# Two low-rank products of a recurrent block put side by side on the array, with half of a projection between them

## The chip, the cores and the metric

The kernel runs on one NeuronCore of a Trainium2 chip. The metric is the time of one execution on the device in microseconds (us). A profile is one execution in which every instruction's start and length were recorded. PE is TensorE (PEld its weight loads), DVE is VectorE, ACT is ScalarE, POOL is GpSimd, SP is SyncE, whose queue starts nearly all transfers.

## What is computed

A model of two blocks in a row, float32 throughout, 256 tokens of width 1024. The second block has a layer of attention, a mixture of 32 experts, a recurrent layer (RWKV-7 time mixing) and a second mixture of experts. The change lies in the first part of the recurrent layer. Cut to what matters:

```python
def rwkv7_time_mix(x, mu, w_rkv, w_o, w0, w1, w2, a0, a1, a2, g1, g2, k_k, k_a, r_k, ...):
    xx = jnp.pad(x, ((0, 0), (1, 0), (0, 0)))[:, :-1] - x
    xm = x[None] + xx[None] * mu[:, None, None, :]            # six mixed inputs
    r, k, v = jnp.einsum('nbsd,nde->nbse', xm[:3], w_rkv)     # 1024 -> 1024 each
    xv, xw, xa, xg = xm[2], xm[3], xm[4], xm[5]
    w = -jax.nn.softplus(-(w0 + jnp.tanh(xw @ w1) @ w2)) - 0.5   # decay: 1024 -> 64 -> 1024
    a = jax.nn.sigmoid(a0 + (xa @ a1) @ a2)                      # learning rate: 1024 -> 64 -> 1024
    g = jax.nn.sigmoid(xg @ g1) @ g2                             # gate: 1024 -> 160 -> 1024
    kk = (k * k_k).reshape(B, S, H, N)
    kk = kk / jnp.maximum(jnp.sqrt(jnp.sum(kk * kk, -1, keepdims=True)), 1e-12)
    k = k * (1.0 + (a - 1.0) * k_a)
    ...                                                       # then the recurrence over time
```

## The kernel before

One instruction stream for each engine is written out by hand, in the order in which it runs. `tensor_program`, `vector_program`, `scalar_program`, `gpsimd_program` and `sync_program` each have a function `rwkv` or a part for this layer. Engines wait for each other by counting semaphores: an instruction that ends something others need gets a name ("rw lw1"), and `wait_ge(*act("rw lw1"))` waits until ACT has come to that name. Nothing is reordered: an engine that waits holds up all that stands behind in its stream.

**PSUM.** TensorE's results go to four tiles of 128 x 1024 (ps0 to ps3), which are handed out in turn by `tile(name, ...)`. The tile handed out is waited for until the engine that reads its former content has done so. Each "half" of a product (512 of the 1024 outputs, as four blocks of 128 outputs by 256 tokens) fills one such tile.

**The stretch in question on TensorE (before).** k0, k1 (the k projection, two halves of 32 matmuls 128x128 by 128x256) come first. Then "rw w" is 8 matmuls of 128 inputs by 64 outputs on the array's columns 0 to 63. "rw a" is 8 alike on columns 64 to 127. Then come the second factors, "rw lw0", "rw lw1" (decay, 64 inputs on the array's rows 0 to 63) and "rw aT0", "rw aT1" (learning rate, rows 64 to 127), with four matmuls each. Then r0 and r1 (the r projection), the sums of squares "rw norm", the gate's first factor "rw g", the product "rw kk0/kk2" which spreads the norms, the gate's second factor "rw gt0/gt1", "rw bon", and half of the v projection, "rw v0". One fp32 matmul makes two MATMUL records in the trace.

**ACT.** It copies k0, k1; takes tanh of w and copies a into `r.loT`; scales k into `r.kk` by 8 instructions; then 16 sigmoids (lw0, lw1, aT0, aT1, four each); copies r0 and r1; takes the square root of the norms ("rw ln"); the gate's sigmoids; three exponentials; and further copies.

**DVE.** It makes the mixed inputs (`mix(i, dst)`: 8 instructions each). mix 0 (for r) overwrites the buffer `r.xa` from which k is computed, so it waits for "rw k1". mix 5 and mix 2 overwrite the inputs of w and a. Then, in its stream in this order:

```python
        v.wait_ge(*act("rw aT1"))
        for k in range(KT):
            ts(ka3[:, k, :], aT[:, k, :], vcol("ka", k), r.om[:, k:k + 1], MUL, ADD)
        tt(flat(kT), v_, flat(kT), MUL)
        for k in range(KT):
            after_own()
            v.tensor_tensor_scan(Lc[:, k, :], tab["rst"], lw[:, k, :], 0.0, MUL, ADD).then_inc(*dve.one())
        tt(flat(lw), flat(Lc), flat(lw), SUB, "rw decay")
        ln = xx[:, 0:2, :]
        v.wait_ge(*pe("rw norm"))
        ts(ln, two(ps("rw norm"), 256), 1e-24, None, MAX, None, "rw norm")
        v.wait_ge(*act("rw ln"))
        rec(ln, ln, "rw ln")
```

TensorE's "rw kk0" waits for this last "rw ln" of DVE.

Of the kernel before, what the change touches and what calls it, by code (L numbers as in the profile page):

```python
# [13 lines left out]
P = 128  # L14
# [3 lines left out]
KT = 8  # L18
# [379 lines left out]
def tensor_program(t, m):  # L398
# [3 lines left out]
    ps = m.ps  # L402
    ps.restart()

    def mm(lst, name=None):
        for n, (o, l, r, first, last) in enumerate(lst):
            i = t.matmul(o, l, r, start=first, stop=last, skip_group_check=True)  # L407
            if n == len(lst) - 1:
                i.then_inc(*pe.one(name))
# [14 lines left out]
    def tile(name, *free):  # L424

        p, old = ps.take(name, *free)
        for engine, done in old:
            t.wait_ge(*engine(done))
        return p
# [642 lines left out]
    def rwkv():  # L1072
# [4 lines left out]
            tr([(p[:, (k % 4) * 256 + i * P:(k % 4) * 256 + i * P + P], x[:, i, k * P:(k + 1) * P], idn)  # L1077
                for k in range(4 * half, 4 * half + 4) for i in range(NT)], n)

        def proj(name, ready, src):  # L1080
            for half in range(2):
                n = f"rw {name}{half}"
                p = tile(n, (act, n))
                t.wait_ge(*m.w.landed(n))
                t.wait_ge(*dve(ready))
                mm(proj_T(wcols(m.w(n), KT, 512), src, KT, [(p[:, c * 256:(c + 1) * 256], slice(c * P, (c + 1) * P)) for c in range(4)]), n)
# [5 lines left out]
        p = tile("rw wa", (act, "rw wa out"))  # L1092
        t.wait_ge(*m.w.landed("rw lora1"))
        t.wait_ge(*dve("rw mix3"))
        mm([(p[0:64, 0:256], lv[:, k, 0:64], r.xb[:, k, :], k == 0, k == 7) for k in range(KT)], "rw w")
        t.wait_ge(*dve("rw mix4"))
        mm([(p[64:128, 512:768], lv[:, k, 64:128], r.xc[:, k, :], k == 0, k == 7) for k in range(KT)], "rw a")
        for base, n_ in ((0, "lw"), (64, "aT")):
            for half in range(2):
                n = f"rw {n_}{half}"  # L1100
                p = tile(n, (act, n))
                t.wait_ge(*act("rw wa out"))
                t.wait_ge(*m.w.landed("rw lora2"))
                mm([(p[:, c * 256:(c + 1) * 256], lora2[base:base + 64, (4 * half + c) * P:(4 * half + c + 1) * P],
                     r.loT[base:base + 64, :], True, True) for c in range(4)], n)
        proj("r", "rw mix0", r.xa)
        sq3 = flat(r.gt).rearrange("p (k s) -> p k s", k=KT)
        p = tile("rw norm", (dve, "rw norm"))
        t.wait_ge(*dve("rw kk2"))
# [217 lines left out]
def vector_program(v, m):  # L1327
# [591 lines left out]
    def rwkv():  # L1919
# [19 lines left out]
        ka3 = v_.rearrange("p (k s) -> p k s", k=KT)  # L1939
        v.wait_ge(*act("rw kk"))  # L1940
        tt(g_, flat(kk), flat(kk), MUL, "rw kk2")
        v.wait_ge(*pe("rw w"))
        mix(5, r.xb)
        v.wait_ge(*pe("rw a"))
        mix(2, r.xc)
        ts(r.om, m.vec[:, m.VO["ka"]:m.VO["ka"] + 8], -1.0, 1.0, MUL, ADD)
        v.wait_ge(*act("rw aT1"))
# [152 lines left out]
def scalar_program(s, m):  # L2100
# [351 lines left out]
    def rwkv():  # L2452
        r = m.rw
        B = blocks(m)
        s.wait_ge(*pe("rw in0"))
        cp(m.hT[:, 0:4, :], ps("rw in0").rearrange("p (k s) -> p k s", k=4), "rw in0 out")

        def proj_out(name, dst):
            for half in range(2):
                n = f"rw {name}{half}"  # L2460
                s.wait_ge(*pe(n))
                cp(dst[:, 4 * half:4 * half + 4, :], ps(n).rearrange("p (k s) -> p k s", k=4), n)

        proj_out("k", r.kT)
        p = ps("rw wa")
        s.wait_ge(*pe("rw w"))
        fn(r.loT[0:64], p[0:64, 0:256], ACT.Tanh)
        s.wait_ge(*pe("rw a"))
        cp(r.loT[64:128], p[64:128, 512:768], "rw wa out")
        for k in range(KT):  # L2470
            fn(r.kk[:, k, :], r.kT[:, k, :], ACT.Copy, "rw kk" if k == KT - 1 else None, scale=vcol("kk", k))
        for n_, dst, bias in (("lw", r.lw, "w0"), ("aT", r.aT, "a0")):
            for half in range(2):
                n = f"rw {n_}{half}"
                s.wait_ge(*pe(n))
                for c in range(4):
                    fn(dst[:, 4 * half + c, :], ps(n)[:, c * 256:(c + 1) * 256], ACT.Sigmoid, n if c == 3 else None,
                       bias=vcol(bias, 4 * half + c))
        proj_out("r", r.rT)
        ln, sg = r.xx[:, 0:2, :], r.xx[:, 2:4, :]  # L2480
        s.wait_ge(*dve("rw norm"))
        fn(ln, ln, ACT.Sqrt, "rw ln")
        p = ps("rw g")
        s.wait_ge(*pe("rw g"))
        s.wait_ge(*dve("rw mix2"))
        fn(sg[:, 0, :], p[:, 0:256], ACT.Sigmoid)
        fn(sg[0:32, 1, :], p[0:32, 256:512], ACT.Sigmoid, "rw g out")
        dec = -math.exp(-0.5)
        s.wait_ge(*dve("rw decay"))
        fn(flat(r.vt), flat(r.Lc), ACT.Exp, "rw e1", scale=dec)  # L2490
        fn(flat(r.xb), flat(r.Lc), ACT.Exp, "rw e3", scale=-dec)
        fn(flat(r.lw), flat(r.lw), ACT.Exp, "rw e2", scale=dec)
        for i in range(NT):
            s.wait_ge(*pe(f"rw gt{i}"))
            cp(r.gt[:, i, :], ps(f"rw gt{i}"), f"rw gt{i}")
        s.wait_ge(*dve("rw pc"))
        for half in range(2):
            n = f"rw v{half}"
            s.wait_ge(*pe(n))
            cp(r.vt[:, :, 512 * half:512 * half + 512], ps(n).rearrange("p (t n) -> p t n", t=NT), n)  # L2500

        def out(i, n, dst, mark=" out"):
            s.wait_ge(*pe(f"rw{i} {n}"))
            cp(dst, ps(f"rw{i} {n}"), f"rw{i} {n}{mark}")

        def powers(i, step):

            s.wait_ge(*pe(f"rw{i} pw{step} d"))
            out(i, f"pw{step} n", B[i]["n"])
            out(i, f"pw{step} d", B[i]["d"])  # L2510

        for i in range(NT):
            s.wait_ge(*pe(f"rw{i} sq d"))
            s.wait_ge(*m.pool(f"rw{i} X"))
            out(i, "sq n", B[i]["n"])
            out(i, "sq d", B[i]["d"])
        for i in range(NT):
            powers(i, 1)
        for i in range(NT):
            out(i, "mv", B[i]["mv"])  # L2520
        for i in range(NT):
            powers(i, 2)
        for i in range(NT):
            out(i, "T0 n", B[i]["n"])
            out(i, "T0 d", B[i]["d"])
        for i in range(NT):
            out(i, "ktok", B[i]["ktok"], "")
        for i in range(NT):
            out(i, "T1", B[i]["n"])
        for i in range(NT):  # L2530
            out(i, "atok", B[i]["atok"], "")
            out(i, "btok", B[i]["btok"], "")
        for i in range(NT):
            out(i, "U", B[i]["U"])
        for i in range(NT):
            s.wait_ge(*pe(f"rw{i} G"))
            w = 1024 >> i
            cp(B[i]["G"][:, 0:w], ps(f"rw{i} G")[:, 0:w], f"rw{i} G")
        for i in range(NT):
            out(i, "y0", m.hb[:, i, :], "")  # L2540

        def rms(i):
            s.wait_ge(*dve(f"rw o{i} ms"))
            fn(r.va[i], r.va[i], ACT.Sqrt, f"rw o{i} rms")

        for i in range(NT):
            rms(i)
            tile_out(f"rw oT{i}", r.kT, i)
        join("rw", range(NT))
# [325 lines left out]
```

## Time and profile before

| | |
|---|---|
| median of 3 runs | 2208.9 us (2207.1 to 2209.21) |
| the profiled execution: its own time | 2207.6 us |
| its span, first to last instruction | 2205.7 us |
| PE busy | 1796.1 us, 81% of the span |
| DVE busy | 603.0 us, 27% |
| ACT busy | 392.2 us, 18% |
| mean granted TensorE clock | 0.917 of full |

Busy time is the time in which an engine has an instruction in work. The span leaves out some 2 us of launch and end, which the own time has. The stretch in question begins 1399 us after the span's start.

### The profile page before, as it was taken

What the parts mean: (1) busy time and instruction counts of PE and PEld (TensorE: products, weight loads), DVE (VectorE), ACT (ScalarE), POOL (GpSimd) and SP (SyncE); (2) the same over time, 40 slices, a digit from 0 to 9 for tenths busy, and PEclk for the clock granted to TensorE, in tenths of its full rate; (3) what the DMA queues carried; (4) which work ended last, traced back from release to release, by engine and by line L of the source; (5) the groups of instructions that cost most, each with busy time, mean ns of one, the idle gap of its engine ahead of it and who ended that gap; (6) DMA issues with size and microseconds to landing.
All of it is one profiled execution on the core that took longest, in us unless ns stands there. A gap on an engine that the chain in (4) does not pass through costs nothing.

```text
span 2205.7 us, 30929 instructions
## 1 busy us (share of the span) xinstructions
PE 1796.1 (81%) x13574; PEld 1129.6 (51%) x13574; DVE 603.0 (27%) x1013; ACT 392.2 (18%) x755; POOL 16.9 (1%) x18
## 2 busy tenths in 40 slices
PE   6999999999999987675766887699986677966663
PEld 4788884878886754222222332575983322322220
DVE  1133312123422145211111212464345321121102
ACT  2233211323301142100000001141221100100001
POOL 0000000000000000000000000001000000000000
PEclk9999999999999998988798998799997788989877
DMA  9322333333234434899999996213013899999995
GB/s 337 104 81 96 134 145 151 123 82 129 96 134 172 171 115 196 367 425 425 425 425 425 425 373 244 77 57 116 4 50 128 367 424 425 413 424 425 424 426 223
DMA packets 51162, 539.55 MB, mean 245 GB/s; under 512 B 7392, under 2 KB 16224, under 8 KB 17664
## 3 DMA queue, kind: packets, MB, share of 16 engines
q1 hardware_dynamic: 49248, 527.06, 58.7%
q0 software_dynamic: 864, 6.29, 0.8%
q8 instruction: 173, 2.83, 0.5%
q10 hardware_dynamic: 832, 3.00, 0.4%
q14 instruction: 45, 0.37, 0.0%
HBM read 535.28 MB, written 1.05 MB: 243 GB/s over the span
## 4 chain that ended last, share of the span: by engine, by line
PE 69%; DMA 18%; DVE 5%; issue 5%; ACT 3%; DVEq 0%; ACTq 0%
PE ps L407 53%; PE ps L414 13%; DMA arena<-in_moe_w_gu 10%; DMA arena<-in_moe_w_down 3%; DMA ring<-in_moe_w_down 3%; PE ps L420 3%; DMA ring<-in_moe_w_gu 1%; DVE x L1350 1%; ACT arena L2121 1%; DVE arena L1339 1%; ACT hb L2117 1%; DVE mT L1339 1%; ACT arena L2392 0%; ACT arena L2117 0%; DVE mT L1912 0%
## 5 line engine op out<-in xcount | busy, mean ns | idle before, releaser
L407 PE MATMUL ps<-hT,ring 128*128 128x256 f32 (+2 forms) x1888 | 392.5, 372 | 0.0
L407 PEld LDWEIGHTS ps<-hT,ring 128*128 128x128 f32 (+2 forms) x1888 | 330.8, 185 | 54.0 <-issue 3.4
L414 PE MATMUL ps<-arena 128*32 128x512 f32 (+1 forms) x1572 | 242.7, 703 | 107.5 <-issue 68.8
L414 PE MATMUL ps<-ring,arena 128*32 128x512 f32 x1472 | 210.6, 708 | 99.9 <-issue 72.9
L2121 ACT ACTIVATE arena<-ps 128x512 f32<-128x512 f32 (+4 forms) x143 | 93.4, 653 | 894.7 <-PE ps L414 518.5
L407 PE MATMUL ps<-arena 64*64 64x64 f32 (+10 forms) x1944 | 184.2, 320 | 57.0 <-ACT arena L2392 22.3
L1339 DVE TENSOR_TENSOR arena<-arena,ps 128x256 f32<-128x256 f32 (+2 forms) x82 | 46.0, 561 | 558.7 <-ACT arena L2117 466.6
L414 PEld LDWEIGHTS ps<-arena 128*32 128x32 f32 (+1 forms) x1572 | 64.0, 130 | 261.6 <-issue 204.2
L407 PEld LDWEIGHTS ps<-arena 64*64 64x64 f32 (+4 forms) x1944 | 113.5, 159 | 130.5 <-ACT arena L2392 52.8
L414 PEld LDWEIGHTS ps<-ring,arena 128*32 128x32 f32 x1472 | 54.8, 126 | 237.4 <-issue 194.2
L407 PE MATMUL ps<-ring,hT 128*128 128x256 f32 (+4 forms) x576 | 148.6, 416 | 8.7 <-ACT hT L2117 7.0
L407 PE MATMUL ps<-arena,ring 64*64 64x64 f32 (+2 forms) x1120 | 140.3, 299 | 10.8 <-DVE arena L1350 8.3
L407 PE MATMUL ps<-ring,arena 64*64 64x64 f32 (+3 forms) x1328 | 128.3, 310 | 13.7 <-issue 8.9
L407 PEld LDWEIGHTS ps<-arena,ring 64*64 64x64 f32 (+2 forms) x1120 | 122.5, 163 | 26.7 <-DVE arena L1350 8.7
L407 PEld LDWEIGHTS ps<-ring,hT 128*128 128x128 f32 x576 | 98.9, 192 | 50.8 <-issue 27.7
L1339 DVE TENSOR_TENSOR mT<-mT,ps 128x1024 f32<-128x1024 f32 x40 | 48.8, 1221 | 209.3 <-PE ps L407 209.2
L407 PEld LDWEIGHTS ps<-ring,arena 64*64 64x64 f32 (+3 forms) x1328 | 72.7, 137 | 62.6 <-issue 57.2
L407 PE MATMUL ps<-ring,mT 64*64 64x64 f32 (+1 forms) x704 | 73.5, 286 | 0.6 <-issue 0.6
L420 PE MATMUL ps<-tcom,arena 128*128 128x128 f32 (+1 forms) x370 | 53.8, 281 | 24.5 <-ACT arena L2121 24.5
L420 PEld LDWEIGHTS ps<-tcom,arena 128*128 128x128 f32 (+1 forms) x370 | 42.2, 143 | 61.5 <-issue 57.2
L2117 ACT ACT_TABLE_LOAD x50 | 64.2, 1283 | 44.7 <-DVE small L1344 18.8
L407 PE MATMUL ps<-arena,x 128*128 128x128 f32 x512 | 70.7, 298 | 1.5 <-DVE arena L1339 1.5
(162 smaller groups left out, 1231.2 us busy)
## 6 DMA issues: line engine op xcount, KB each, us to landing
ring<-in_moe_w_gu SPq DMA_DIRECT2D x64, 2048.0 KB, 28.6
arena<-in_moe_w_gu SPq DMA_DIRECT2D x64, 2048.0 KB, 30.9
arena<-in_moe_w_down SPq DMA_DIRECT2D x32, 2048.0 KB, 32.9
ring<-in_moe_w_down SPq DMA_DIRECT2D x32, 2048.0 KB, 31.5
ring<-in_w_merge SPq DMA_DIRECT2D x16, 2048.0 KB, 7.7
ring<-in_w_in SPq DMA_DIRECT2D x10, 2048.0 KB, 7.3
ring<-in_attn_w_qkv SPq DMA_DIRECT2D x6, 2048.0 KB, 7.5
ring<-in_rw_w_rkv SPq DMA_DIRECT2D x6, 2048.0 KB, 7.5
```

The source lines that it names most:

```text
L407: i = t.matmul(o, l, r, start=first, stop=last, skip_group_check=True)
L414: i = t.matmul(o, l, r, start=first, stop=last, skip_group_check=True)
L420: i = t.transpose(o, a, e)
L1339: v.tensor_tensor(o, a, b, op).then_inc(*dve.one(name))
L1350: v.scalar_tensor_tensor(out=o, in0=a, scalar=s, in1=b, op0=op0, op1=op1).then_inc(*dve.one(name))
L2117: s.activation(o, a, f, **k).then_inc(*act.one(name))
L2121: s.activation(o, a, ACT.Copy).then_inc(*act.one(name))
```

## The change

On TensorE: the 16 matmuls of w and a alternate between the two halves of the array's columns, under one name "rw wa". r0 comes right behind them. Then lw0 and aT0 are handed two tiles at once, and their matmuls alternate between the two halves of the rows; then lw1 and aT1 the same way; then r1. DVE and ACT wait for "rw wa" where they waited for "rw w" and "rw a". ACT takes its work in a new order: copy r0, sigmoids lw0 and aT0, copy r1, sigmoids lw1 and aT1.

```diff
-        def proj(name, ready, src):
-            for half in range(2):
+        def proj(name, ready, src, halves=range(2)):
+            for half in halves:
...
         p = tile("rw wa", (act, "rw wa out"))
         t.wait_ge(*m.w.landed("rw lora1"))
         t.wait_ge(*dve("rw mix3"))
-        mm([(p[0:64, 0:256], lv[:, k, 0:64], r.xb[:, k, :], k == 0, k == 7) for k in range(KT)], "rw w")
         t.wait_ge(*dve("rw mix4"))
-        mm([(p[64:128, 512:768], lv[:, k, 64:128], r.xc[:, k, :], k == 0, k == 7) for k in range(KT)], "rw a")
-        for base, n_ in ((0, "lw"), (64, "aT")):
-            for half in range(2):
-                n = f"rw {n_}{half}"
-                p = tile(n, (act, n))
-                t.wait_ge(*act("rw wa out"))
-                t.wait_ge(*m.w.landed("rw lora2"))
-                mm([(p[:, c * 256:(c + 1) * 256], lora2[base:base + 64, (4 * half + c) * P:(4 * half + c + 1) * P],
-                     r.loT[base:base + 64, :], True, True) for c in range(4)], n)
-        proj("r", "rw mix0", r.xa)
+
+        mm([o for k in range(KT) for o in ((p[0:64, 0:256], lv[:, k, 0:64], r.xb[:, k, :], k == 0, k == 7),
+                                           (p[64:128, 512:768], lv[:, k, 64:128], r.xc[:, k, :], k == 0, k == 7))], "rw wa")
+        proj("r", "rw mix0", r.xa, (0,))
+        for half in range(2):
+
+            ns = [f"rw {n_}{half}" for n_ in ("lw", "aT")]
+            ps_ = [tile(n, (act, n)) for n in ns]
+            t.wait_ge(*act("rw wa out"))
+            t.wait_ge(*m.w.landed("rw lora2"))
+            mm([(o[:, c * 256:(c + 1) * 256], lora2[base:base + 64, (4 * half + c) * P:(4 * half + c + 1) * P],
+                 r.loT[base:base + 64, :], True, True) for c in range(4) for base, o in zip((0, 64), ps_)], ns[0])
+            pe.name(ns[1])
+        proj("r", "rw mix0", r.xa, (1,))
...
         tt(g_, flat(kk), flat(kk), MUL, "rw kk2")
-        v.wait_ge(*pe("rw w"))
+        v.wait_ge(*pe("rw wa"))
         mix(5, r.xb)
-        v.wait_ge(*pe("rw a"))
         mix(2, r.xc)
...
         p = ps("rw wa")
-        s.wait_ge(*pe("rw w"))
+        s.wait_ge(*pe("rw wa"))
         fn(r.loT[0:64], p[0:64, 0:256], ACT.Tanh)
-        s.wait_ge(*pe("rw a"))
         cp(r.loT[64:128], p[64:128, 512:768], "rw wa out")
         for k in range(KT):
             fn(r.kk[:, k, :], r.kT[:, k, :], ACT.Copy, "rw kk" if k == KT - 1 else None, scale=vcol("kk", k))
-        for n_, dst, bias in (("lw", r.lw, "w0"), ("aT", r.aT, "a0")):
-            for half in range(2):
+        def r_out(half):
+            n = f"rw r{half}"
+            s.wait_ge(*pe(n))
+            cp(r.rT[:, 4 * half:4 * half + 4, :], ps(n).rearrange("p (k s) -> p k s", k=4), n)
+
+        for half in range(2):
+            r_out(half)
+            for n_, dst, bias in (("lw", r.lw, "w0"), ("aT", r.aT, "a0")):
                 n = f"rw {n_}{half}"
                 s.wait_ge(*pe(n))
                 for c in range(4):
                     fn(dst[:, 4 * half + c, :], ps(n)[:, c * 256:(c + 1) * 256], ACT.Sigmoid, n if c == 3 else None,
                        bias=vcol(bias, 4 * half + c))
-        proj_out("r", r.rT)
         ln, sg = r.xx[:, 0:2, :], r.xx[:, 2:4, :]
```

The order on ACT before, from the 8 scalings of k to the square root ("rw ln", 128x512). The rows of 128x256 from ps are the sigmoids of lw0, lw1, aT0 and aT1, four each; the two of 128x1024 are the copies of r0 and r1.

```order
L2117 ACTIVATE arena<-arena,vec 128x256 [waits act_done] x8
L2117 ACT_TABLE_LOAD [waits act_done]
L2117 ACTIVATE arena<-ps,vec 128x256 [waits pe_done]
L2117 ACTIVATE arena<-ps,vec 128x256 [waits act_done] x3
L2117 ACTIVATE arena<-ps,vec 128x256 [waits act_done,pe_done]
...
L2121 ACTIVATE arena<-ps 128x1024 [waits act_done,pe_done] x2
L2117 ACT_TABLE_LOAD [waits act_done]
L2117 ACTIVATE arena<-arena 128x512 [waits dve_done]
```

The same place on ACT after the change: the copy of r0, the table load, the sigmoids of lw0 and aT0, the copy of r1, and those of lw1 and aT1.

```order
L2119 ACTIVATE arena<-arena,vec 128x256 [waits act_done] x8
L2123 ACTIVATE arena<-ps 128x1024 [waits act_done,pe_done]
L2119 ACT_TABLE_LOAD [waits act_done]
L2119 ACTIVATE arena<-ps,vec 128x256 [waits pe_done]
...
L2119 ACTIVATE arena<-ps,vec 128x256 [waits act_done] x3
L2123 ACTIVATE arena<-ps 128x1024 [waits act_done,pe_done]
L2119 ACTIVATE arena<-ps,vec 128x256 [waits act_done,pe_done]
...
L2119 ACTIVATE arena<-ps,vec 128x256 [waits act_done] x3
L2119 ACT_TABLE_LOAD [waits act_done]
L2119 ACTIVATE arena<-arena 128x512 [waits dve_done]
```

One copy (r1) now stands ahead of eight of the sixteen sigmoids, and one (r0) ahead of them all; the number of table loads is as before.

On TensorE before, from the a product to r0, with the numbers of tiles (ps0 to ps3) and of weight buffers:

```order
L407 MATMUL ps0<-hb,ring0 64x256 x7
L407 MATMUL ps1<-arena,ring1 128x256 [waits ring_landed1,act_done,dve_done]
L407 MATMUL ps1<-arena,ring1 128x256 x3
L407 MATMUL ps2<-arena,ring1 128x256 [waits ring_landed1,act_done]
L407 MATMUL ps2<-arena,ring1 128x256 x3
L407 MATMUL ps3<-arena,ring1 128x256 [waits ring_landed1,act_done]
L407 MATMUL ps3<-arena,ring1 128x256 x3
L407 MATMUL ps0<-arena,ring1 128x256 [waits ring_landed1,act_done]
L407 MATMUL ps0<-arena,ring1 128x256 x3
L407 MATMUL ps1<-arena,ring2 128x256 [waits dve_done,ring_landed2,act_done]
L407 MATMUL ps1<-arena,ring2 128x256 x31
```

On TensorE after, from the last of the alternating w and a matmuls to r1; r0 is the one from ring2, r1 the one from ring3:

```order
L407 MATMUL ps0<-mT,ring0 64x256
L407 MATMUL ps0<-hb,ring0 64x256
L407 MATMUL ps1<-arena,ring2 128x256 [waits dve_done,ring_landed2]
L407 MATMUL ps1<-arena,ring2 128x256 x31
L407 MATMUL ps2<-arena,ring1 128x256 [waits act_done,ring_landed1]
L407 MATMUL ps3<-arena,ring1 128x256
...
L407 MATMUL ps0<-arena,ring1 128x256 [waits act_done,ring_landed1]
L407 MATMUL ps1<-arena,ring1 128x256
...
L407 MATMUL ps2<-arena,ring3 128x256 [waits dve_done,ring_landed3,act_done]
L407 MATMUL ps2<-arena,ring3 128x256 x31
```

r0 now takes ps1 and stands ahead of the second factors. lw0 and aT0 take ps2 and ps3, lw1 and aT1 ps0 and ps1, and r1 takes ps2, which it shares in turn with lw0. DVE's order is unchanged. The rows behind r1 (norm on ps3, g on ps0, kk0 on ps1, kk2 on ps2) are as before.

## Rows read from the trace of the kernel before

**Rows 1.** Chain that ended last, in the window 1380 to 1550 us: start, us, what.

```profile
1399.04 0.14 issue
1399.18 36.69 PE ps L407 x160
...
1444.01 67.20 PE ps L407 x424
```

**Rows 2.** Timeline of PE: start, us, engine, line, operation, records, [idle before, releaser].

```profile
1399.18 30.43 PE L407 MATMUL ps<-arena,ring 128*128 128x256 f32 x128 [8.34 <-DVE arena L1350]
...
1436.37 6.39 PE L407 MATMUL ps<-arena,ring 64*128 64x256 f32 x32 [0.52 <-issue]
1444.01 27.89 PE L407 MATMUL ps<-arena,ring 128*128 128x256 f32 x128 [1.25 <-ACT arena L2117]
1471.83 1.07 PE L407 MATMUL ps<-arena,tcom 128*32 128x256 f32 x16
1472.83 7.29 PE L407 MATMUL ps<-mT,ring 128*128 128x256 f32 x32
1480.06 1.16 PE L407 MATMUL ps<-arena,tcom 32*128 32x256 f32 x16
...
1493.21 15.62 PE L407 MATMUL ps<-ring,hb 128*128 128x512 f32 x32
```

**Rows 3.** Timeline of PE where w ends and a begins.

```profile
1429.54 3.02 PE L407 MATMUL ps<-mT,ring 128*64 128x256 f32 x13
...
1432.39 0.38 PE L407 MATMUL ps<-mT,ring 128*64 128x256 f32 x1
1432.45 0.38 PE L407 MATMUL ps<-hb,ring 128*64 128x256 f32 x1
1432.61 0.38 PE L407 MATMUL ps<-mT,ring 128*64 128x256 f32 x1
```

**Rows 4.** Timeline of ACT from the scalings of k to the square root.

```profile
1436.30 4.29 ACT L2117 ACTIVATE arena<-arena,vec 128x256 f32<-128x256 f32 x8
1440.67 1.28 ACT L2117 ACT_TABLE_LOAD   x1
1441.96 8.26 ACT L2117 ACTIVATE arena<-ps,vec 128x256 f32<-128x256 f32 x16
...
1471.94 1.02 ACT L2121 ACTIVATE arena<-ps 128x1024 f32<-128x1024 f32 x1 [12.79 <-PE ps L407]
...
1474.33 0.63 ACT L2117 ACTIVATE arena<-arena 128x512 f32<-128x512 f32 x1
```

**Rows 5.** Timeline of DVE from mix 0 to the end of its preparations.

```profile
1429.65 4.13 DVE L1350 SCALAR_TENSOR_TENSOR arena<-arena,vec,hT 128x256 f32<-128x256 f32 x8 [22.28 <-PE ps L407]
...
1451.69 3.56 DVE L1346 TENSOR_SCALAR arena<-arena,vec 128x256 f32<-128x256 f32 x8
...
1463.41 2.29 DVE L1339 TENSOR_TENSOR arena<-arena 128x2048 f32<-128x2048 f32 x1
1472.97 0.69 DVE L1344 TENSOR_SCALAR arena<-ps 128x512 f32<-128x512 f32 x1 [7.27 <-PE ps L407]
1474.99 3.35 DVE L1358 RECIPROCAL arena<-arena 128x512 f32<-128x512 f32 x1 [1.33 <-ACT arena L2117]
...
1497.83 2.29 DVE L1350 SCALAR_TENSOR_TENSOR arena<-arena 128x2048 f32<-128x2048 f32 x1
```

**Rows 6.** Windows: stretch, its length, busy by engine, PE clock, DMA share, GB/s.

```profile
1399.20:1404.40 5.20, 5.20 (x12) 4.16 (x13) 4.84 (x11) 0.00 (x0) 0.00 (x0) 0.50 0.01 3
1404.40:1429.50 25.10, 25.10 (x117) 21.85 (x115) 2.79 (x6) 1.02 (x1) 0.00 (x0) 1.00 0.22 84
1493.10:1496.50 3.40, 3.40 (x6) 1.61 (x7) 3.37 (x2) 0.00 (x0) 0.00 (x0) 0.50 0.88 376
```

**Rows 7.** The second mixture of experts: its window, in the same columns.

```profile
1700.00:2180.00 480.00, 333.93 (x2298) 131.68 (x2301) 93.29 (x187) 39.65 (x73) 0.00 (x0) 0.85 0.98 412
```

**Rows 8.** Timeline of SP's queue where those experts' transfers start.

```profile
1698.84 0.92 SPq L2634 DMA_DIRECT2D arena<-in_moe_w_down  x2
```

## Prediction

> **What bounds the kernel now.** I read first the chain of work that ended last, in the window of the recurrent layer. It is nearly all TensorE: 36.69 us from 1399.18, and 67.20 us without a break from 1444.01 [rows 1]. Between the two it goes over ACT: the copy of a, the scalings of k, the table load and the four sigmoids of lw0, for whose tile r0 waits [rows 4], while TensorE works through its 6.39 us of second factors [rows 2]. So a microsecond less or more of TensorE here moves all that follows. Behind the layer, the second mixture of experts runs with the transfers at 0.98 of their capacity [rows 7], and its stream starts at 1698.84 [rows 8], when the recurrent layer is over and its memory is lent. Nothing upstream of that waits for transfers, so a shift of the layer's end shifts the stream and the end of the kernel by the same amount. I then read the timelines of PE, ACT and DVE, since the change moves only instructions. On PE the reader is to see the stages in a row with gaps of 0.52 and 1.25 us [rows 2]. On ACT the 16 sigmoids run in one piece long before the r copies [rows 4]. On DVE a block of work that needs these sigmoids, the factor of k and the decay's running sums, runs from 1451.69 to 1465.70, followed by 7.27 us of waiting for the norms [rows 5]. That wait is the cushion between the sigmoids and TensorE's product kk0, which began at 1480.06 [rows 2].
>
> **The change on TensorE, up to r1.** Where w ends and a begins, the two happen to run together: w's records start at 1432.39 and 1432.61, a's at 1432.45 between them [rows 3]. That is a pair every 0.22 us, where r takes 27.89 us for 128 records, 0.218 each [rows 2]. So 16 records of w and 16 of a in pairs take 16 x 0.218 = 3.5 us, from 1429.54 to about 1433.1, where they ended at 1399.18 + 36.69 = 1435.87 before [rows 1]. r0 is next. It needs mix 0, which DVE ends at 1429.65 + 4.13 = 1433.78 [rows 5]; with 0.14 us between the end of a mix and a matmul, as ahead of k0 [rows 1], r0 starts at 1433.9. This is a new wait of 0.8 us, but the old one of 0.52 us for ACT's copy goes. Its 64 records end at 1433.9 + 13.95 = 1447.9. The 32 records of the second factors took 6.39 us [rows 2]; on two halves of the rows I take 16 pairs at 0.218, 3.5 us, until 1451.4. `r.loT` is long done by then, since ACT needs only a tanh and a copy for it behind 1433.1. The nearest row for different rows at once is kk0/kk2, 16 records on four row groups in 1.16 us [rows 2], which are 0.07 us each, so the pairing is not in doubt.
>
> r1 takes ps2, so it waits for ACT's sigmoids of lw0. ACT first copies r0 (1448.0 to 1449.1), then loads its table for 1.28 us (before, the load ran at 1440.67 right behind the scalings; now the copy stands ahead of it), then does four sigmoids of 0.516 us, 8.26/16 [rows 4]: done at 1452.5. So r1 starts at 1452.6, after 1.2 us of waiting, as much as the 1.25 us there was. It ends at 1452.6 + 13.95 = 1466.5, against 1471.9 before. **So far TensorE has won 5.4 us.**
>
> **What the new order on ACT does.** The copy of r1 now stands ahead of the sigmoids of lw1 and aT1. These two are ready in PSUM at 1451.4, but ACT waits for r1 until 1466.6, copies for 1.02 us, and does eight sigmoids of 0.516 us: lw1 is done at 1469.8, aT1 at 1471.8. Before, all 16 were done at 1441.96 + 8.26 = 1450.22 [rows 4]. The last one is 21.6 us later. Two things queue behind it.
>
> First, DVE. Its stream waits for aT1 before the block that took 14.0 us (1451.69 to 1463.41 + 2.29 [rows 5]). It now runs from 1471.9 to 1485.9. Only behind it stand the norms, although TensorE has them at 1467.6: 0.69 us for the maximum, ACT's root of 0.63 us [rows 4], and the reciprocal of 3.35 us [rows 5]. With some 0.04 us at each handover, that is 1486.6, 1487.3 and 1490.7. TensorE's kk0 starts at 1490.8 instead of 1480.06: **10.7 us later**.
>
> Second, TensorE itself. norm needs 1.07 us until 1467.6. g takes ps0, which lw1 had, and waits for ACT until 1469.8, 2.2 us, then runs 7.29 us until 1477.1 [rows 2]. Then TensorE is idle for 13.7 us, until 1490.8. The 2.2 us cost nothing since they lie inside that wait.
>
> Nothing behind kk is late in its turn. DVE needs 1500.12 - 1480.06 = 20.1 us from kk0's start to the end of its preparations (1497.83 + 2.29 [rows 5]), while TensorE goes through gt, bon and v0 for 28.8 us, until 1493.21 + 15.62 = 1508.83 [rows 2]. Both move by the same amount, so 8.7 us of cover remain. ACT's exponentials need DVE's decay, which at 1485.9 is ready 4.9 us before kk0 starts, and they stand behind the gate's sigmoids as before. v0's weights are asked for when g is done, at 1477, and are used at 1504. The root's table load stands behind the sigmoids and ends at 1473.2, before the norms come.
>
> **The clock.** A long idle time costs again behind it. After 8.34 us of idle with little before, k0 began at a granted clock of 0.50 (1.2 GHz) until 1404.40, then 1.00 (2.4 GHz) [rows 6]. The same 128 records took 30.43 us there and 27.89 in r [rows 2]: 2.5 us. An idle time of 13.7 us is nearer to that than to the 1.25 us ahead of r, which cost nothing, so I take 2.5 us for kk and gt. The bounds: nothing from below, and from above 2.5 plus another such stretch of 3.4 us at half clock, as at 1493.1 behind bon [rows 6], worth 1.7 us. That one is there already; it might also be missed, -1.7.
>
> **Sum.** 10.7 + 2.5 = 13.2 us later. Against the profiled execution's own 2207.6 us that is 2220.8; the median of the runs, 2208.9, lies 1.3 us above that execution, so 2222. The bounds are 10.7 - 1.7 = 9.0 (2218) and 10.7 + 2.5 + 1.7 = 14.9 (2224), and some 1.5 to 3 us for how the second experts' 480 us fall on the clock.
>
> **A rule that speaks against the pairs.** The row shows w's and a's matmuls, both on all 128 rows and on different columns, started 0.06 us apart [rows 3]. The Trainium skill, "TensorE: Matmul & The Clock Gate", Part 3, says that a weight load overlaps a running matmul only when the row groups differ. By that rule w and a would not run together, while the second factors would. By rows, w and a one after the other take 32 x 0.218 = 7.0 us and end at 1436.5, 2.7 us later than 1433.8, where r0 could start; all behind moves along, 15.9 us in all, 2225. The rule is contradicted by the trace of this case, so I give this 3 in 100.
>
> **Rivals.**
> The forecast, a stall of TensorE before kk because aT1's sigmoids stand behind r1: 2222, 0.84. Its own range is 2217 to 2226.
> (A) The gain arrives: kk0 starts right behind g. Then norm, g end at 1466.5 + 1.07 + 7.29 = 1474.8, 5.3 us earlier than 1480.1, 2204. For it speaks only that TensorE is the chain and wins 5.4 us. From aT1's end to kk0 DVE and ACT need 1490.8 - 1471.8 = 19.0 us, so aT1 would have to be done by 1455.8 for the whole gain, and 1461.1 is the point from which the time is not longer than before. ACT reaches aT1 at 1471.8 because the r1 copy is ahead of it. 0.03.
> (B) The stall is there but absorbed behind, by a wait that is there anyway: 2209, no change. Against it: the chain in the layer is unbroken TensorE [rows 1], and transfers of the experts start only when the layer ends [rows 8]. 0.04.
> (C) The pairs don't form, by the rule above: 2225, 0.03.
> (D) The stall takes more with it, a second slow-clock stretch in gt and v0, or later wait of DVE's: from 17 us, 2227 and more, 0.06.
>
> **How the numbers follow.** A run of this kernel differs from another by some 2 us, so within 0.2% (4.4 us) counts as no change. Faster has only (A), 0.03. The same has (B), 0.04. Slower has the rest, 0.93. The range 2217 to 2227 holds the forecast and (C); left out are A, B, most of D and the forecast's edge, together under 2 in 10.
>
> **What the changed profile would show.** w's and a's records alternate in pairs 0.22 us apart and r0 starts near 1433.9; the second factors take 3.5 us. r1 begins near 1452.6 with a wait of about 1.2 us for ACT. On ACT there is an idle time of some 12 us ahead of the second 128x1024 copy, with eight sigmoids behind it. DVE idles some 20 us until 1471.9, ahead of its 128x256 TENSOR_SCALARs. PE idles some 13.7 us before the 32-row matmuls at 1490.8, and the granted clock there is 0.5 for a few microseconds. The experts' transfers start near 1712. It would be wrong if ACT came to aT1 before r1, if DVE's norms did not stand behind the decay block, or if later waits shrank by as much as this one costs.

## Result, and the profile after

| | median | lowest to highest | runs |
|---|---|---|---|
| before | 2208.94 us | 2207.1 to 2209.21 | 4 |
| changed | 2230.58 us | 2227.95 to 2236.78 | 4 |

The ratio is 1.0104, with an interval of 1.008 to 1.0128: 21.6 us slower. On another chip, beside the experiments, it was 2227.05 us against 2206.82, ratio 1.0086 (1.0064 to 1.0108). The forecast was slower by 13, to 2222, and its range ended at 2227. The profiled execution took 2236.78 us, the longest of the four, with a span of 2234.8.

PE's timeline of the changed kernel, in the columns of [rows 2] (w's and a's last two records stand here for their 32):

```profile
1401.32 30.42 PE L407 MATMUL ps<-arena,ring 128*128 128x256 f32 x128 [8.34 <-DVE arena L1353]
...
1434.96 0.38 PE L407 MATMUL ps<-mT,ring 128*64 128x256 f32 x1
1434.97 0.38 PE L407 MATMUL ps<-hb,ring 128*64 128x256 f32 x1
1436.06 17.71 PE L407 MATMUL ps<-arena,ring 128*128 128x256 f32 x96 [0.71 <-DVE arena L1353]
1454.59 14.08 PE L407 MATMUL ps<-arena,ring 128*128 128x256 f32 x64 [0.82 <-ACT arena L2119]
1468.60 1.07 PE L407 MATMUL ps<-arena,tcom 128*32 128x256 f32 x16
1471.87 7.29 PE L407 MATMUL ps<-mT,ring 128*128 128x256 f32 x32 [2.20 <-ACT arena L2119]
1492.93 2.22 PE L407 MATMUL ps<-arena,tcom 32*128 32x256 f32 x16 [13.77 <-DVE arena L1361]
1495.08 16.10 PE L407 MATMUL ps<-ring,arena 128*128 128x512 f32 x16
1511.10 6.99 PE L407 MATMUL ps<-tcom,arena 128*128 128x2 f32 x32
```

The whole layer started 2.14 us later in this execution (k0 at 1401.32, before at 1399.18 [rows 2]), so places are compared from k0's start on. The reader is to see the three waits, 0.71 for mix 0, 0.82 for lw0's sigmoids and 2.20 for lw1's, and then 13.77 us of idle time ahead of kk0. Behind it everything takes nearly twice its time: kk 2.22 us for 1.16, gt 16.10 for 8.50, bon 6.99 for 3.78.

ACT's timeline there, where the copy of r1 stands between the two groups of eight sigmoids:

```profile
1450.15 1.02 ACT L2123 ACTIVATE arena<-ps 128x1024 f32<-128x1024 f32 x1 [9.65 <-PE ps L407]
1451.25 1.28 ACT L2119 ACT_TABLE_LOAD   x1
1452.54 4.08 ACT L2119 ACTIVATE arena<-ps,vec 128x256 f32<-128x256 f32 x8
1468.70 1.02 ACT L2123 ACTIVATE arena<-ps 128x1024 f32<-128x1024 f32 x1 [12.08 <-PE ps L407]
1469.82 4.08 ACT L2119 ACTIVATE arena<-ps,vec 128x256 f32<-128x256 f32 x8
```

And DVE's, from the block that waits for them to the reciprocal, against [rows 5]:

```profile
1473.93 3.56 DVE L1349 TENSOR_SCALAR arena<-arena,vec 128x256 f32<-128x256 f32 x8 [22.50 <-ACT arena L2119]
...
1485.65 2.29 DVE L1342 TENSOR_TENSOR arena<-arena 128x2048 f32<-128x2048 f32 x1
1488.05 0.69 DVE L1347 TENSOR_SCALAR arena<-ps 128x512 f32<-128x512 f32 x1
1489.43 3.35 DVE L1361 RECIPROCAL arena<-arena 128x512 f32<-128x512 f32 x1 [0.69 <-ACT arena L2119]
```

DVE waits 22.50 us for the sigmoids and no longer at all for the norms; the 7.27 us of cushion are gone. Windows of the changed kernel, in the columns of [rows 6]: g, the idle time, kk, gt, bon, and v0 up to and from the return of the clock.

```profile
1471.90:1479.10 7.20, 7.20 (x32) 4.60 (x32) 4.88 (x9) 3.18 (x5) 0.00 (x0) 1.00 0.01 2
1479.10:1492.90 13.80, 0.06 (x1) 0.00 (x0) 12.58 (x12) 3.91 (x5) 0.00 (x0) 0.59 0.40 152
1492.90:1495.00 2.10, 2.07 (x16) 1.52 (x16) 0.00 (x0) 2.06 (x3) 0.00 (x0) 0.50 0.00 0
1495.00:1511.10 16.10, 16.10 (x19) 4.00 (x16) 15.26 (x15) 4.74 (x3) 0.00 (x0) 0.50 0.00 0
1511.10:1517.90 6.80, 6.80 (x33) 6.80 (x33) 2.72 (x2) 1.02 (x1) 0.00 (x0) 0.50 0.80 308
1517.90:1522.60 4.70, 4.70 (x7) 2.12 (x8) 0.19 (x1) 0.00 (x0) 0.00 (x0) 0.50 0.00 0
1522.60:1534.20 11.60, 11.60 (x31) 4.88 (x31) 0.00 (x0) 0.00 (x0) 0.00 (x0) 1.00 0.00 0
```

The clock column stays at 0.50 through kk, gt, bon and the start of v0, 29.7 us from kk0's start, although TensorE is busy all that time. The forecast had some 5 us of it.

### The profile page after: what moved, and what is told of

Read it like the earlier page. It is cut to its first block, busy times and chain, and to the rows that moved or that the text cites. A ratio compares the mean times of both kernels' runs of the same rounds, so it can differ in the third digit from the quotient of the medians.

```text
span 2234.8 us, 30928 instructions
## 1 busy us (share of the span) xinstructions
PE 1815.6 (81%) x13574; PEld 1134.4 (51%) x13574; DVE 602.9 (27%) x1013; ACT 392.0 (18%) x755; POOL 16.9 (1%) x18
## 3 DMA queue, kind: packets, MB, share of 16 engines
HBM read 535.28 MB, written 1.05 MB: 240 GB/s over the span
## 4 chain that ended last, share of the span: by engine, by line
PE 67%; DMA 19%; DVE 6%; issue 5%; ACT 3%; DVEq 0%; ACTq 0%
PE ps L407 52%; PE ps L414 12%; DMA arena<-in_moe_w_gu 8%; DMA arena<-in_moe_w_down 6%; DMA ring<-in_moe_w_down 3%; PE ps L420 2%; DMA ring<-in_moe_w_gu 1%; DVE x L1353 1%; DVE arena L1342 1%; ACT arena L2123 1%; ACT hb L2119 1%; DVE mT L1342 1%; DVE arena L1353 1%; ACT arena L2394 0%; ACT arena L2119 0%
## 5 line engine op out<-in xcount | busy, mean ns | idle before, releaser
L407 PE MATMUL ps<-ring,arena 64*64 64x64 f32 (+3 forms) x1328 | 138.0, 325 | 12.6 <-issue 8.0
L407 PEld LDWEIGHTS ps<-ring,hT 128*128 128x128 f32 x576 | 100.7, 195 | 53.4 <-issue 30.5
L1365 DVE COPY arena<-ps 128x512 f32<-128x512 f32 (+7 forms) x60 | 36.3, 605 | 126.5 <-PE ps L407 116.3
```

The costliest lines, as they stand in the source:

```text
L1365: v.tensor_copy(o, a).then_inc(*dve.one(name))
```

## The experiments

Two theories stood at the outset. The first: aT1's sigmoids behind r1 make kk0 10.7 us late, and the slow clock which the idle time leaves makes up the rest. The rival: something else of the change costs, the pairs or a shift in the second experts. All profiles are put side by side here; the places count from k0's start (before: 1399.18). Medians are against the runs of before on the same chip: 2206.75 for e1 to e4, 2206.82 for e5 to e9, 2205.7 for e10 to e12, and 2208.94 for the first row of the changed kernel.

| kernel | idle ahead of kk0 | kk0 starts | from kk0 to v0 | oT0 starts | median, change to before |
|---|---|---|---|---|---|
| before | 0 | 80.9 | 13.2 | 263.7 | |
| changed (first profile) | 13.8 | 91.6 | 25.0 | 290.6 | +21.6 |
| e9 changed again | 13.8 | 91.6 | 25.0 | 289.8 | +20.2 |
| e1 sigmoids first | 2.95 | 78.5 | 23.6 | 273.6 | +2.6 |
| e2 pairs only | 0 | 80.4 | 15.7 | 266.4 | +3.1 |
| e3 filler | 0 | 90.4 | 14.8 | 278.9 | +19.9 |
| e10 filler, wide | 0 | 93.6 | 14.8 | 283.6 | +15.8 |
| e4 v0 ahead of gt | 13.8 | 90.5 | | 279.2 | +17.3 |
| e8 idle time alone | 3.41 | 84.7 | 25.0 | 280.3 | +15.4 |
| e7 pairs undone | 2.65 | 80.4 | 15.8 | 266.4 | +1.0 |
| e5 norms early | 0 | 75.5 | 14.5 | 259.6 | -5.5 |
| e12 the same, no pairs | 0 | 77.7 | 13.4 | 262.6 | -3.6 |

(e4 has v0 elsewhere. oT0 are the transposes that end the recurrence. The rows behind this table are PE's timelines of each kernel. In e3 and e4 the 128 records of k0 and k1 took 29.3 us instead of 30.4, so their places are some 1.1 us early in this count.)

The last column does not follow from the one ahead of it alone. From oT0 to the end of the span these profiles took 539.7 to 543.1 us, e3 546.5, in no order that follows the edits, and k0 itself started between 1396.0 and 1401.3. So a microsecond in the layer is read from the places, and a median is asked only for more than that.

**e1, the sigmoids ahead of r1's copy.**

```diff
-        for half in range(2):
-            r_out(half)
+        r_out(0)
+        for half in range(2):
             for n_, dst, bias in (("lw", r.lw, "w0"), ("aT", r.aT, "a0")):
...
+        r_out(1)
```

> The change with one thing undone: ACT does all 16 sigmoids ahead of the copy of r1 (the copy of r0 stays first). Theory (the loss comes from aT1's sigmoids standing behind r1 on ACT, and from the slow clock that the stall leaves): aT1 is done near 1456.7 us on the time axis of before, DVE's decay block ends at 1470.7, the norms and the reciprocal follow, kk0 starts at 1475.6 right behind g, without a long idle time and at full clock. 1475.6 against 1480.06: 4.5 us faster than before, about 2204.5. Rival (the pairs on the array or r0's new place cost something by themselves): slower than before by several us even so.

Measured: 2209.31 us (2200.91 to 2225.09, 12 runs), ratio 1.0014 (0.9993 to 1.0035): the large loss is gone with this one edit, but no gain was seen. Part of the number was my own slip: 16 sigmoids, not 8, stand between the table load and DVE, so aT1 is done at 1458.7, not 1456.7, and kk0 started at 78.5, which is 1477.7 on the axis of before and still 2.4 us early. But it started behind 2.95 us of idle time, and what follows is the surprise. PE's timeline and the windows of e1:

```profile
1478.73 1.27 PE L407 MATMUL ps<-arena,tcom 32*128 32x256 f32 x16 [2.95 <-DVE arena L1361]
1479.93 15.59 PE L407 MATMUL ps<-ring,arena 128*128 128x512 f32 x16
```

```profile
1478.70:1480.50 1.80, 1.77 (x18) 1.20 (x18) 0.60 (x1) 1.79 (x2) 0.00 (x0) 0.99 0.94 400
1480.50:1507.80 27.30, 27.30 (x55) 12.74 (x54) 17.57 (x17) 6.03 (x5) 0.00 (x0) 0.50 0.27 104
```

The clock fell 0.6 us into gt and stayed at half for 27.3 us of uninterrupted matmuls. From kk0 to v0 that is 23.6 us for 13.2, so this execution should end 10.4 - 2.4 = 8.0 us later than before, and its own time, 2215.32 us, is 8.6 above the median of before. The 24 us of spread over 12 runs would fit some runs with this and some without, but only the profiled one can be seen.

**e2, the pairs alone.** Before, with the two alternating lists, r0 and r1 behind them and ACT in its old order.

```diff
+        mm([o for k in range(KT) for o in ((p[0:64, 0:256], lv[:, k, 0:64], r.xb[:, k, :], k == 0, k == 7),
+                                           (p[64:128, 512:768], lv[:, k, 64:128], r.xc[:, k, :], k == 0, k == 7))], "rw wa")
...
+                 r.loT[base:base + 64, :], True, True) for c in range(4) for base, o in zip((0, 64), ps_)], ns[0])
...
         proj("r", "rw mix0", r.xa)
```

> The kernel before with the alternating w and a, and the alternating lw and aT, alone; r0 and r1 behind them and ACT's order as before. Theory: the pairs save 2.7 and 3 us of TensorE's time, but r0 waits for ACT's sigmoids of lw0, which follow the eight scalings of k and the table load; ACT starts these 2.1 us sooner (1434.2 instead of 1436.3). So r0 starts 2.1 us sooner and the kernel is 2 us faster, 2207, and TensorE idles some 4 us ahead of r0. Rival (pairs as such are slow): no gain or a loss.

Measured: 2209.82 us, ratio 1.0012 (1.0003 to 1.0021), 3.1 us slower. r0 waited 3.76 us for ACT, as expected, and started 2.2 us sooner. But clock was lost behind the wait: r took 29.58 us instead of 27.89, at half clock for its first 3.4 us. bon was 2.6 us longer too: the clock fell at 1489.1, inside it, and came back at 1499.4, where before it fell at bon's end and for 3.4 us. What TensorE's time the pairs save did not reach the total.

**e3 and e10, the stall filled.** Both keep the late kk0 and take away TensorE's idle time.

```diff
             p = tile(f"rw kk{n0}", (dve, f"rw kk{n0} out"))
+            if n0 == 0:
+                mm([(p[:, 0:256], tab["one"], x[:, k % 2, 0:256], True, True) for k in range(31)])
             t.wait_ge(*dve("rw ln"))
```

> The changed kernel plus 31 matmuls of 128x128 by 128x256 on data of no use behind g, into the tile that kk0 overwrites: 13.4 us of TensorE work inside its idle time of 13.8 us ahead of kk0. They feed nothing. Theory (10.7 us of the loss are the late kk0, the rest is the slow clock that follows the idle time): the clock stays full through kk, gt and bon, kk0 starts at the same place, and the loss is 10.7 us alone, 2219.6. Rival (the rest is lost elsewhere, for instance in the second experts): 2230 as with the change, or 2231.

> The changed kernel with filler in the stall again, now 16 matmuls of 128x128 by 128x512 instead of 31 of 256 columns: the same 13.8 us of TensorE's time with half as many instructions more. They feed nothing. Theory (late kk0 10.7 us, the rest the clock; the first filler's extra loss came from TensorE's own instruction waits, 3.88 us in the pair products where before had 1.48): full clock through kk and gt, kk0 10.9 us late, no longer instruction waits than before, and 2206.8 + 12 = 2219. Rival (the loss of 19.9 us with the first filler has another cause than the number of instructions): 2226 again.

Measured: e3 2226.61 us, ratio 1.0096 (1.008 to 1.0111); e10, with 16 of 512 columns, 2221.53, ratio 1.0071 (1.0058 to 1.0085). The point they were made for is clear in the profiles: with kk0 as late as in the changed kernel, gt took 8.50 us instead of 16.10 and the way from kk0 to v0 14.8 us instead of 25.0. PE's timeline of e10, and a window of kk and gt:

```profile
1475.69 14.00 PE L407 MATMUL ps<-x,tcom 128*128 128x512 f32 x32
1489.62 1.16 PE L407 MATMUL ps<-arena,tcom 32*128 32x256 f32 x16
1490.70 8.50 PE L407 MATMUL ps<-ring,arena 128*128 128x512 f32 x16
...
1527.45 0.34 PE L407 MATMUL ps<-arena 64*64 64x64 f32 x8 [3.65 <-issue]
```

```profile
1489.60:1499.10 9.50, 9.50 (x33) 3.12 (x32) 7.71 (x11) 5.14 (x4) 0.00 (x0) 1.00 0.00 0
```

So 10.2 us of the loss between kk0 and v0 come from the idle time by way of the clock. The totals came out higher than I had written, though, and e3's, +19.9 beside +20.2 for the changed kernel, shows no gain at all: the 10.2 us rest on the profiles, where oT0 starts 10.9 us sooner in e3 and 6.2 us sooner in e10 than in e9. In both, TensorE stood idle longer in the products behind v0, for nothing that the profile shows (3.88 and 3.65 us of "issue", before 1.5), and the clock dipped for 3.4 us once more behind it. My thought that half as many added instructions would shorten this wait fell: it was 3.65 against 3.88. In e10 there was a dip in g too (8.86 us instead of 7.29, behind its 2.2 us wait), which put kk0 2.0 us later. And e3 took 3.8 us longer than before from oT0 to the end. Why is open.

**e4, v0 ahead of gt.**

```diff
+        values(0)
         sg = r.xx[:, 2:4, :]
         for i in range(NT):
             p = tile(f"rw gt{i}", (act, f"rw gt{i}"))
```

> The changed kernel with the first half of the v projection (32 records of 128x128 by 128x512, dense) moved from behind bon to ahead of gt. Theory (the clock is given back after a stretch of dense matmuls and is not given back by gt, which alternates 128 and 32 rows, nor by bon with 2 columns): the clock is full again about 5 us behind kk0, gt runs at full clock, and the time is 2208.9 + 10.7 + 2.6 = 2222. Rival (the clock stays low for a length of time whatever runs): 2230, as with the change.

Measured: 2224.04 us, ratio 1.0071 (1.0056 to 1.0086), +17.3. Behind the same 13.8 us of idle time the clock was back 4.5 us behind kk0's start, and gt, bon and most of v0 ran at full clock, in all 29.7 us from kk0 to the end of the three, where the changed kernel has 41.2 and before 28.7:

```profile
1493.60:1496.00 2.40, 2.40 (x5) 1.18 (x4) 2.30 (x2) 2.37 (x2) 0.00 (x0) 0.50 0.00 0
1496.00:1517.00 21.00, 21.00 (x47) 7.82 (x45) 15.65 (x15) 2.29 (x2) 0.00 (x0) 1.00 0.00 0
```

So the clock does not stay low for a set time; what runs matters. The total is above 2222, and one cause is to be seen: the clock fell again at 1519.9, inside bon, which now stands just ahead of the small products, and these ran at half clock until 1530.2.

**e11, gt dense.** It leaves out gt's second factor and takes the first one twice. Its total can't be compared, since the gate's values are others, and from oT0 to the end it took 41 us longer than before; I take it that the experts there get other tokens, which no run tests.

```diff
-                for n in range(2) for a, b, first in ((sg[:, 0, :], g2a, True), (sg[0:32, 1, :], g2b, False))], f"rw gt{i}")
+                for n in range(2) for a, b, first in ((sg[:, 0, :], g2a, True), (sg[:, 0, :], g2a, False))], f"rw gt{i}")
```

> The changed kernel with gt's second factor left out: its 32-row matmuls are replaced by a repeat of the 128-row ones, so the gate's values are not the reference's. As many matmuls of as many columns, all on 128 rows. Theory (gt does not bring the clock back because half of its matmuls use 32 rows in turn with 128): the clock is full again within 6 us behind kk0's start, during gt, and the time is 2206.8 + 10.7 + 3 + some 1.5 for bon = 2222 or, since gt loses its changes of rows, 2220. Rival (gt does not bring the clock back for another reason, or none comes back before a set time): half clock into v0 as with the change, 2227.

Measured: 2255.39 us, ratio 1.0221 (1.0206 to 1.0235). In the layer the answer is plain. PE's timeline and windows of e11:

```profile
1490.09 2.22 PE L407 MATMUL ps<-arena,tcom 32*128 32x256 f32 x16 [12.21 <-DVE arena L1361]
1492.24 9.05 PE L407 MATMUL ps<-ring,arena 128*128 128x512 f32 x16
```

```profile
1492.20:1496.10 3.90, 3.90 (x7) 1.80 (x6) 3.58 (x5) 3.67 (x2) 0.00 (x0) 0.50 0.00 0
1496.10:1501.10 5.00, 5.00 (x12) 2.14 (x12) 4.72 (x7) 1.02 (x1) 0.00 (x0) 1.00 0.00 0
```

With all 16 records on 128 rows the clock came back 3.9 us into gt, behind 12.2 us of idle time. With every second matmul on 32 rows it did not in 16.1 us of gt, nor in bon. The edit changes two things at once: it takes away the 32 rows, and with them the changes of shape, which cost time of their own (two records of 512 columns start every 1.05 us in gt at full clock, and every 0.86 in e11). Which of the two holds the clock down was not tried apart.

**e8, an idle time and nothing else.** The kernel before, with four instructions on DVE that only take time.

```diff
         v.wait_ge(*act("rw ln"))
+        for _ in range(4):
+            tt(xx[:, 4:8, :], xx[:, 4:8, :], xx[:, 4:8, :], MIN)
         rec(ln, ln, "rw ln")
```

> The kernel before, with nothing of the change, and four idle-making instructions of 1.23 us on DVE (minimum of a free buffer with itself) ahead of the reciprocal, so that kk0 starts about 3.3 us later, behind as much idle time of TensorE. Theory (a short idle time ahead of kk can drop the clock, and neither kk nor gt nor bon brings it back): half clock from kk into v0 in the profile, and a median well above 3.3 us later, up to 14 us, with a wide spread of the runs. Rival (an idle time costs its length): 3.3 us later, runs as close together as before.

Measured: 2222.22 us, ratio 1.0077 (1.006 to 1.0095): 15.4 us for 3.41 us of idle time. kk0 was 3.8 us late and the way from kk0 to v0 25.0 us, 11.9 longer, exactly as in the changed kernel:

```profile
1478.10:1481.50 3.40, 0.05 (x1) 0.00 (x0) 3.31 (x1) 3.20 (x4) 0.00 (x0) 0.96 0.69 226
1481.50:1506.60 25.10, 25.05 (x65) 12.40 (x65) 17.98 (x16) 6.62 (x5) 0.00 (x0) 0.50 0.35 136
```

This needs nothing of the change: 3.8 us late and 11.9 us of clock are 15.7 us, for 15.4 measured. So the rival is not needed for the clock's part of the loss.

**e9, the changed kernel again.**

> The changed kernel again, beside the others on one chip. Theory: 21.6 us slower than before, as first measured, within 3 us.

Measured: 2227.05 us, +20.2, with the same 13.78 us of idle time and 16.10 us of gt.

**e7, pairs undone, e1 otherwise.**

```diff
+        mm([(p[0:64, 0:256], lv[:, k, 0:64], r.xb[:, k, :], k == 0, k == 7) for k in range(KT)])
+        mm([(p[64:128, 512:768], lv[:, k, 64:128], r.xc[:, k, :], k == 0, k == 7) for k in range(KT)], "rw wa")
...
+            for base, o, n in zip((0, 64), ps_, ns):
+                mm([(o[:, c * 256:(c + 1) * 256], lora2[base:base + 64, (4 * half + c) * P:(4 * half + c + 1) * P],
+                     r.loT[base:base + 64, :], True, True) for c in range(4)], n)
```

> The first experiment's kernel with both pairs undone: w then a, lw0 then aT0, lw1 then aT1, each in one piece; r0's place and ACT's order stay. Theory (the pairs are worth 2.7 + 3 us of TensorE's time up to g's end): r1 ends at 1471.3, g at 1479.6, kk0 at 1479.9 with 0.3 us of idle time, so the same time as before within 1 us and full clock in gt. Rival (the pairs are worth nothing): r1 and g end where they do with the pairs, near 1474.8.

Measured: 2207.77 us, ratio 1.0009 (0.9995 to 1.0022). kk0 started at 80.4, 0.5 us sooner than before, behind 2.65 us of idle time. g ended only 2.2 us later than in e1 with the pairs (77.8 and 75.6 from k0's start), not 5. Part of the reason is in the two waits that the pairs open: with them TensorE waits 0.71 us for mix 0 and 0.83 us for lw0's sigmoids, and without them r0, the second factors and r1 are one piece of 160 records in 32.93 us. That is 0.206 for a record, less than r's 0.218. I take it that one row half hands over to the other early between lw0, aT0, lw1 and aT1, as w does to a at [rows 3]; the records don't show it one by one.

This profile also holds an exception to what e1 and e8 show:

```profile
1476.59 2.21 PE L407 MATMUL ps<-arena,tcom 32*128 32x256 f32 x16 [2.65 <-DVE arena L1360]
1478.74 9.04 PE L407 MATMUL ps<-ring,arena 128*128 128x512 f32 x16
```

The granted clock fell to 0.50 at 1476.5, just ahead of kk0, and was back at 1.00 at 1479.9, 1.1 us into gt, the same gt with 32 rows in turn. In e8 it fell 0.3 us ahead of kk0 instead of 0.1, and stayed low for 30.7 us. What decides between the two is open.

**e5, the norms early.** e1, and on DVE:

```diff
+        v.wait_ge(*act("rw lw1"))
+        for k in range(KT):
+            after_own()
+            v.tensor_tensor_scan(Lc[:, k, :], tab["rst"], lw[:, k, :], 0.0, MUL, ADD).then_inc(*dve.one())
+        tt(flat(lw), flat(Lc), flat(lw), SUB)
         v.wait_ge(*act("rw aT1"))
         for k in range(KT):
             ts(ka3[:, k, :], aT[:, k, :], vcol("ka", k), r.om[:, k:k + 1], MUL, ADD)
-        tt(flat(kT), v_, flat(kT), MUL)
...
         rec(ln, ln, "rw ln")
+        tt(flat(kT), v_, flat(kT), MUL, "rw decay")
```

> The first experiment's kernel (sigmoids ahead of the r1 copy) with DVE's work reordered: running sums and decay as soon as lw1 is there, then the factor of k, then the norms and the reciprocal, and the product with k after them. aT1 is done at 1458.7 us on the time axis of before, the decay at 1464.8, the factor at 1468.4, the reciprocal at 1473.2; g ends on TensorE at 1474.8, so kk0 follows it without idle time. Theory (kk0's place and the idle time ahead of it decide, the latter through the clock): 5.2 us faster than before, kk0 at 1474.9, full clock through gt in every run, so runs as close together as those of before. Rival (the slow clock in gt comes from the pairs or from something else in the change and not from the idle time): slow clock in gt again, and no gain.

Measured: 2201.31 us (2197.32 to 2205.39, 12 runs), ratio 0.9979 (0.9967 to 0.9991): 5.5 us faster than before, as written. kk0 started at 75.5, which is 1474.7, with no idle time and full clock through gt (it fell at 1486.9, inside bon, for 6.8 us):

```profile
1468.04 7.29 PE L407 MATMUL ps<-mT,ring 128*128 128x256 f32 x32
1475.26 1.16 PE L407 MATMUL ps<-arena,tcom 32*128 32x256 f32 x16
1476.35 8.50 PE L407 MATMUL ps<-ring,arena 128*128 128x512 f32 x16
```

**e12, the same without the pairs.** e5 with e7's edit on TensorE.

> The fast version (sigmoids ahead of r1's copy, norms early on DVE) with both pairs undone. In the profiles g ended 2.1 us later without pairs than with them. Theory: kk0 follows g without idle time, 2.1 us later than in the fast version: 2203.4, full clock in gt. Rival (the pairs carry the whole gain of 5.5 us): 2206.8, as before the change.

Measured: 2202.11 us, ratio 0.9981 (0.9972 to 0.999), 3.6 us faster than before. The rival is out: most of the gain is there without the pairs. Its timeline has no wait for ACT left between a and g, where r0 now stands. In the profiles kk0 is 2.2 us later than with the pairs (77.7 and 75.5); the medians, -3.6 and -5.5, agree with that but overlap in their intervals.

## Why the prediction was wrong

**TensorE up to r1: right.** The pairs ran as pairs. r0 started 34.7 us behind k0 (forecast 1433.9, which is 34.7), r1 at 53.3 (forecast 53.4), each behind the wait that was named (0.71 for 0.8, 0.82 for 1.2). Of the 5.4 us won by then, e7 and e1 show 3.2 from r0's new place, which fills old waits, and 2.2 from the pairs: from w's start to norm's it is 42.3 us before, 39.1 in e7 and 36.9 in e1. On w and a the Trainium skill ("TensorE: Matmul & The Clock Gate", Part 3) is contradicted by the trace: its rule that a weight load overlaps a running matmul only when the row groups differ, read as the prediction read it, would have kept them apart, and their records start 0.01 us apart on the same 128 rows.

**The order on ACT: right.** g waited 2.20 us (2.2), the idle time ahead of kk0 was 13.77 us (13.7), and kk0 started at 91.6 - 80.9 = 10.7 us later (10.7). e1 undoes only this order: the long idle time is gone, and of the medians' loss (21.6 us, 20.2 in e9) 2.6 are left, so the mechanism is shown.

**The clock: this is the step that failed.** It said "so I take 2.5 us for kk and gt", with the first projection as its row, and "from above 2.5 plus another such stretch". It measured 25.02 - 13.15 = 11.9 us more from kk0 to v0, in both profiles of the changed kernel and in e8. I took the recovery behind k0's start, 5.2 us, as a property of the clock (in e3 and e4 k0's own took some 2.9). It goes with what runs, and k0's matmuls all use 128 rows and 128 columns. In both profiles of the changed kernel, in e8 and in e1 gt at half clock did not bring the full one back, and bon neither; v0's dense matmuls did, in the changed kernel 4.7 us behind their start. e11 and e4 show this from both sides, one profile each. e7 is the exception: there the clock was back 1.1 us into gt, so gt can fail to bring it back and need not. The row to distrust was there: the clock had dipped at 1493.1 behind bon [rows 6], so what followed kk was not like k0. With 11.9 in place of 2.5 the sum is 22.6 us, and v0 starts 22.6 us later in both profiles; the medians say 21.6 and 20.2.

**"A long idle time costs again behind it": right, but a short one does too.** The forecast had rows for 8.34 and 1.25 us of idle time and none between. e8 lost 11.9 us by 3.41 us.

**Nothing behind kk is late in its turn: right.** DVE was ahead of TensorE up to the pair products. But more was lost further on: between v1 and oT0 3.9 us in the first profile and 2.6 in the second, each with one more stretch of 6.8 us at half clock, which before does not have. e1 has it too, e5 and e7 have not; its cause is open. So both profiled executions lost more than the sum, 27.0 and 23.1 us from k0 to the end, and lie above their medians; that the sum meets the medians this closely is in part luck.

**Absorption, (B): out.** SP's queue in the changed kernel, where the experts' transfers start:

```profile
1728.03 0.95 SPq L2640 DMA_DIRECT2D arena<-in_moe_w_down  x2
```

That is 29.2 us behind [rows 8], 27.0 against k0's start, and the end came 27.0 us later on the same count.

**Rival (D)** was nearest, at 0.06. It named the second slow stretch in gt, and should have had a price from gt and bon at half clock throughout: 8.5 + 3.8 us once more.

## What to carry to other kernels

When an engine's stream is reordered so that a copy stands ahead of work that was ready, ask what that work feeds: here a copy put in between delayed a DVE block of 14 us and through it TensorE. Price an idle time of TensorE by what stands behind it. If that is dense, a few microseconds of half clock follow (3.4 in e2, 5.2 behind k0's start); if it is thin (few rows in turn, 2 columns) it may run at half clock from end to end, so put a dense product there or close the gap. Pairing small matmuls on halves of the array is worth only what the next wait leaves of it: of 3.7 us of TensorE's time (e1 beside e7) two new waits took 1.5, and 2.2 were left.

## What the runs showed of the hardware

- Granted clock behind idle times ahead of kk, with gt and bon following: 3.41 us (e8) and 2.95 us (e1) were followed by 30.7 and 27.3 us at 1.2 GHz, 2.65 us (e7) by 3.4 us. Where there was none (before, e2, e3, e5, e10, e12), gt ran at 2.4 GHz to its end. Ahead of g, the same 2.2 us of waiting was followed by a slow stretch in e10 and e11 (g 8.86 and 8.87 us) and not in the changed kernel, e9, e3 and e4 (7.29 us). So near 2 to 3 us the outcome differs between runs, and e1's runs spread over 24 us where those of before on that chip spread over 10.
- gt, 16 records of 512 columns with 32 rows in turn, took 8.50 us at full and 16.10 us at half clock. It kept the full clock in the six profiles with no idle time ahead of kk (before, e2, e3, e5, e10, e12), and in e4, where v0 stood ahead of it. At half clock it did not win the full one back in four (changed, e9, e8, and e1, where the clock fell 0.6 us into it), and did in one (e7).
- The clock also falls with no idle time at all. In the eight profiles in which this gt ended at full clock and bon (2 columns) came somewhere behind it, the clock fell inside bon or at its end, for 3.4 us (before, e12), 6.8 (e3, e5, e7, e10) or 10.2 (e2, e4). In e11, with gt on 128 rows throughout, it did not fall there. This is most of the difference between 13.2 (before) and 15.7 us (e2) in the table's column from kk0 to v0.
- Two matmuls on the same rows and different column halves started 0.01 us apart, every 0.216 us a pair. Row pairs are near that: 32 records in 3.72 us (e2).
- In long runs of 64x64 matmuls TensorE stands idle at times for nothing that the profile shows: 1.5 us behind v0 before, 3.9 us with 62 records more ahead (e3) and 3.7 with 32 more (e10). What sets this was not tried.
